# Inverting the recurrent core's triangular blocks by two 64-row quarters of the array instead of one 128-row whole

## What is computed

```
def step(state, inp):
    r_t, w_t, k_t, v_t, kk_t, b_t = inp
    sa = jnp.einsum('bhvk,bhk->bhv', state, -kk_t)
    state = state * w_t[..., None, :] + sa[..., None] * b_t[..., None, :] + v_t[..., None] * k_t[..., None, :]
    return state, jnp.einsum('bhvk,bhk->bhv', state, r_t)
```

## Time and profile before

| | us |
|---|---|
| median of 3 runs (1482.71 to 1483.98) | 1483.03 |
| the profiled execution | 1483.33 |
| its span | 1481.5 |
| recurrent core, chunk 0, first input matmul to right side | 874.02 to 914.14 |
| recurrent core, chunk 1, the same | 926.70 to 966.33 |
| first expert matmul | 1039.83 |
| PE busy in the span | 1421.2 (96%) |

### The profile page before, as it was taken

The page is one execution under the profiler, slowest core; times in us unless marked ns, Lnnn a source line. Parts: engine busy times, 40 slices in busy tenths (PEclk is TensorE's granted clock), DMA queues, the critical chain, the costliest instruction groups (busy, mean ns, idle before and its releaser), DMA issues.

```text
span 1481.5 us, 19431 instructions
## 1 busy us (share of the span) xinstructions
PE 1421.2 (96%) x7478; PEld 1005.4 (68%) x7478; DVE 638.6 (43%) x1060; ACT 543.6 (37%) x814; POOL 446.0 (30%) x302
## 2 busy tenths in 40 slices
PE   8999999999999999999999999998999999999898
PEld 7888888888788888887787679965444344344343
DVE  5664544445664554354158654744222022022021
ACT  6666543445666634334455422212111111111111
POOL 2472544444372544545868220100000000000000
PEclk9999999999999999999999999999999999999999
DMA  7341455454341455456764600128999999999997
GB/s 272 129 164 58 143 206 192 174 202 160 129 164 58 143 193 204 170 191 230 243 226 130 242 0 13 51 114 356 375 430 430 426 428 428 427 428 427 429 424 296
DMA packets 50248, 351.95 MB, mean 238 GB/s; under 512 B 7747, under 2 KB 9679, under 8 KB 25583
## 3 DMA queue, kind: packets, MB, share of 16 engines
q1 hardware_dynamic: 49438, 349.52, 61.0%
q10 hardware_dynamic: 720, 1.20, 0.2%
HBM read 347.78 MB, written 1.07 MB: 235 GB/s over the span
## 4 chain that ended last, share of the span: by engine, by line
PE 74%; DMA 9%; issue 6%; DVE 4%; ACT 3%; POOL 2%; DVEq 1%; SPq 1%; POOLq 0%; ACTq 0%
PE psum L1813 12%; PE psum L1101 10%; PE psum L1103 10%; PE psum L1102 10%; PE psum L1393 8%; DMA ring<-in_w_expert_up 8%; PE psum L1837 5%; PE psum L1395 4%; PE psum L1091 3%; PE psum L1742 2%; PE psum L1752 2%; PE psum L1222 1%; DMA weights_raw<-in_second_w 1%; PE psum L1608 1%; POOL weights_split L913 1%
## 5 line engine op out<-in xcount | busy, mean ns | idle before, releaser
L913 POOL TENSOR_TENSOR weights_split<-weights_raw,weights_split 128x512 fp32r<-128x512 f32 (+2 forms) x253 | 395.7, 1596 | 361.3 <-ACT weights_split L1919 361.2
L1919 ACT ACTIVATE weights_split<-weights_raw 128x2048 fp32r<-128x2048 f32 (+4 forms) x154 | 243.5, 1587 | 254.6 <-PE psum L1103 149.4
L1813 PE MATMUL psum<-ring,arena 128*64 128x512 f32 x960 | 225.0, 594 | 17.6 <-DMA ring<-in_w_expert_up 12.5
L1393 PE MATMUL psum<-h_split,weights_split 128*128 128x512 f32 x512 | 181.2, 398 | 1.4 <-DVE weights_split L913 1.4
L1813 PEld LDWEIGHTS psum<-ring,arena 128*64 128x64 f32 x960 | 72.9, 137 | 145.1 <-issue 141.2
L1101 PE MATMUL psum<-weights_split,h_split 128*128 128x512 f32 (+3 forms) x400 | 152.1, 380 | 6.4 <-POOL weights_split L913 4.9
L1101 PE MATMUL psum<-weights_split,hidden_split 128*128 128x512 f32 (+1 forms) x384 | 151.5, 394 | 0.0
L913 DVE TENSOR_TENSOR weights_split<-weights_raw,weights_split 128x2048 fp32r<-128x2048 f32 (+3 forms) x53 | 119.5, 2259 | 71.2 <-ACT weights_split L1919 69.4
L1103 PE MATMUL psum<-weights_split,h_split 128*128 128x512 f32 (+3 forms) x400 | 149.9, 375 | 0.0
L1102 PE MATMUL psum<-weights_split,h_split 128*128 128x512 f32 (+3 forms) x400 | 149.7, 374 | 0.0
L1103 PE MATMUL psum<-weights_split,hidden_split 128*128 128x512 f32 (+1 forms) x384 | 148.0, 385 | 0.0
(11 more groups left out here) (381 smaller groups left out, 1888.5 us busy)
## 6 DMA issues: line engine op xcount, KB each, us to landing
weights_raw<-in_layer_w SPq DMA_DIRECT2D x94, 1024.0 KB, 4.8
arena<-in_w_expert_down SPq DMA_DIRECT2D x28, 2048.0 KB, 16.5
ring<-in_w_expert_up SPq DMA_DIRECT2D x28, 2048.0 KB, 16.7
ring<-in_w_expert_gate SPq DMA_DIRECT2D x24, 2048.0 KB, 16.3
weights_raw<-in_second_w SPq DMA_DIRECT2D x44, 512.0 KB, 5.1
ring<-in_w_expert_up SPq DMA_DIRECT2D x8, 1024.0 KB, 12.7
arena<-in_w_expert_down SPq DMA_DIRECT2D x16, 512.0 KB, 11.5
arena<-in_w_expert_gate SPq DMA_DIRECT2D x3, 2048.0 KB, 9.2
```

What stands on the lines that cost most here:

```text
L913: ins = eng.tensor_tensor(W.part(j, 1, n)[:, cols], W.raw(j, n)[:, cols], W.part(j, 0, n).bitcast(F32)[:, cols], ALU.subtract)
L1393: pe.matmul(both.rearrange("p (w s) -> p w s", w=2), w[0][:, k, f * P:(f + 1) * P], hTp[:, :, k, :], start=(k == 0), stop=False)
L1813: ins = pe.matmul(bank[half(j), :], xe[h][:, k, half(j)], w[j][:, k, :], start=(k == 0), stop=(k == KD - 1))
L1919: act.activation(W.part(j, 0, w), W.raw(j, w), ACT.Copy).then_inc(W.hi, 1)
```

## The change

The inverse is built for two diagonal blocks of 64 tokens (`HALF`) at once, and the two are joined at the end.

- `T`, `TT` and `X` shrink to 4 heads x 64 columns: rows 0 to 63 hold the upper diagonal block, rows 64 to 127 the lower. Each product over them (`by_blocks`) is eight matmuls of 64 rows by 64 weights columns by 64 columns, alternately on rows and output partitions 0 to 63 and on 64 to 127, into one bank. Each is a quarter of the array; the two lie on its diagonal.
- Turning `T` is now such a matmul with the identity, not a transpose, and is done at every level, the first too.
- `LEVELS` has five entries instead of six. A last step joins the blocks: `XF` (4 matmuls), a last `TT`, and `XT` (4 matmuls); ACT writes the diagonal blocks and DVE the upper right one into `NT`, which then serves L1682 as `TT` served L1642 before.
- Units of the inputs are made for both `par` together, with the matmuls alternating between the two row halves and two banks (`core_inputs`). `N` (`core_diagonals`) makes only the diagonal blocks. `Mak`, `Mrb` and `Mrk` (`LATE_INPUTS`) move behind the `X` and `TT` units of levels 0, 1 and 2, and their masks on DVE likewise.
- POOL's three operations per `par` go; DVE masks `N` and adds the identity itself.

```
-LEVELS = [2 ** i for i in range(1, 7)]
+LEVELS = [2 ** i for i in range(1, 6)]
+HALF = P // 2
+LATE_INPUTS = ("Mak", "Mrb", "Mrk")
...
+                for c in range(PAIRS):
+                    for par in range(2):
+                        r = slice(RW_E * par, RW_E * (par + 1))
+                        ins = pe.matmul(banks[par][:, c * P:(c + 1) * P], left_m[r, c, tok], right_m[r, c, tok], start=True, stop=True)
...
+            def by_blocks(bank, left, right):
+                for c in range(PAIRS):
+                    for rows in blocks:
+                        ins = pe.matmul(bank[rows, at(c)], left(rows, c), right(rows, c), start=True, stop=True)
+                return ins
...
+                def turned_inverse(n, i, m):
+                    bank = units.begin(("TT", 8 * n + i))
+                    units.finish(("TT", 8 * n + i), by_blocks(bank, lambda rows, c: m["T"][rows, c, :], lambda rows, c: ident[rows, rows]))
...
                 for i in range(len(LEVELS)):
                     for par in range(2):
                         n, m = 2 * t + par, core[par]
...
+                        inverse_ready(n, i)
+                        units.wait_emptied(("NT", n))
                         bank = units.begin(("X", 8 * n + i))
...
+                        units.finish(("X", 8 * n + i), by_blocks(bank, lambda rows, c: m["NT"][rows, c, rows], lambda rows, c: m["T"][rows, c, :]))
+                        turned_inverse(n, i, m)
+                    if i < len(LATE_INPUTS):
+                        core_inputs(t, LATE_INPUTS[i])
                     for par in range(2):
                         n, m = 2 * t + par, core[par]
...
+                        units.wait_emptied(("X", 8 * n + i), ("TT", 8 * n + i))
+                        bank = units.begin(("T", 8 * n + i))
+                        units.finish(("T", 8 * n + i), by_blocks(bank, lambda rows, c: m["TT"][rows, c, :], lambda rows, c: m["X"][rows, c, :]))
...
-            eye = ident.unsqueeze(1).to_broadcast([P, PAIRS, P])
-            for n, (t, par) in enumerate(CORE):
-                m = core[par]
-                pool.wait_ge(core_masked, n + 1)
-                pool.tensor_tensor(m["TT"], m["NT"], second("level1T").unsqueeze(1).to_broadcast([P, PAIRS, P]), ALU.mult)
-                pool.tensor_tensor(m["T"], m["T"], eye, ALU.add)
-                pool.drain()
-                pool.tensor_tensor(m["TT"], m["TT"], eye, ALU.add).then_inc(core_start, 1)
...
                 for i in range(len(LEVELS)):
...
+                    level = second("levels")[:, i * HALF:(i + 1) * HALF]
                     for par in range(2):
                         key = ("X", 8 * (2 * t + par) + i)
...
+                        units.emptied_by(key, dve.tensor_tensor(core[par]["X"], bank, every(level), mul), "V")
+                    if i < len(LATE_INPUTS):
+                        masked_inputs(t, LATE_INPUTS[i])
                     for par in range(2):
...
+                        key, a = ("T", 8 * (2 * t + par) + i), core[par]["T"]
+                        units.emptied_by(key, dve.tensor_tensor(a, over_pairs(units.wait_full(key), HALF), a, add), "V")
                     if t == 1:
                         head_norm(0, i)
```

More of the change, by code:

```diff
@@ new lines, in _, with core_diagonals @@
+            blocks = [slice(HALF * b, HALF * (b + 1)) for b in range(2)]
+            at = lambda c: slice(c * HALF, (c + 1) * HALF)
+            def core_diagonals(t):
+                A, B = rwT[0:2]
+                banks = [units.begin(("N", 2 * t + par)) for par in range(2)]
+                for c in range(PAIRS):
+                    for b, rows in enumerate(blocks):
+                        tok = slice(t * P + HALF * b, t * P + HALF * (b + 1))
+                        for par in range(2):
+                            r = slice(RW_E * par, RW_E * (par + 1))
+                            ins = pe.matmul(banks[par][rows, at(c)], A[r, c, tok], B[r, c, tok], start=True, stop=True)
+                            if c == PAIRS - 1 and b == 1:
+                                units.finish(("N", 2 * t + par), ins)
@@ new lines, in _ @@
+                upper, lower = blocks
+                for par in range(2):
+                    n, m = 2 * t + par, core[par]
+                    inverse_ready(n, len(LEVELS))
+                    bank = units.begin(("XF", n))
+                    for c in range(PAIRS):
+                        ins = pe.matmul(bank[lower, at(c)], m["NT"][upper, c, lower], m["T"][upper, c, :], start=True, stop=True)
+                    units.finish(("XF", n), ins)
+                    turned_inverse(n, len(LEVELS), m)
@@ L1611, in value @@
+                for par in range(2):
+                    n, m = 2 * t + par, core[par]
+                    units.wait_emptied(("XF", n), ("TT", 8 * n + len(LEVELS)))
+                    bank = units.begin(("XT", n))
+                    for c in range(PAIRS):
+                        ins = pe.matmul(bank[upper, at(c)], m["X"][lower, c, :], m["NT"][lower, c, lower], start=True, stop=True)
+                    units.finish(("XT", n), ins)
                 def value(c, par):
@@ L2782, in gate_rw, with masked_inputs @@
                 dve.tensor_tensor(a, a, g, add).then_inc(mixed, 1)
-            every = lambda name: second(name).unsqueeze(1).to_broadcast([P, PAIRS, P])
+            every = lambda table: table.unsqueeze(1).to_broadcast([P, PAIRS, table.shape[1]])
+            over_pairs = lambda bank, w: bank[:, 0:PAIRS * w].rearrange("p (c s) -> p c s", c=PAIRS)
+            def masked_inputs(t, name):
+                for par in range(2):
+                    bank = over_pairs(units.wait_full((name, 2 * t + par)), P)
+                    mask = second("minus_strict" if name in ("NT", "Mak") else "incl")
+                    units.emptied_by((name, 2 * t + par), dve.tensor_tensor(core[par][name], bank, every(mask), mul), "V")
@@ L2785, in _ @@
             for t in range(T):
+                if t == 0:
+                    gate_att(0)
                 for par in range(2):
[L2787 to L2799, removed]
+                    bank = over_pairs(units.wait_full(("N", 2 * t + par)), HALF)
+                    units.emptied_by(("N", 2 * t + par), dve.tensor_tensor(core[par]["T"], bank, every(second("minus_level1")[:, 0:HALF]), mul), "V")
@@ L2838, in _ @@
             gate_rw(1)
-            for step in range(3, len(LEVELS)):
+            for step in range(3, len(LEVELS) + 1):
                 head_norm(1, step)
```

126 lines of the change are left out of this document (67 added, 59 removed).

## The result

The changed kernel takes 1470.88 us (median of 4, 1465.70 to 1472.43) against 1482.87 (4, 1481.12 to 1483.98): a ratio of 0.9909, 95% interval 0.9889 to 0.9930. Repeated beside the last experiments it took 1471.25 (6) against 1482.08 (12), 0.9920 (0.9904 to 0.9937). So it is faster by 12 us, inside the range of 1456 to 1474 but outside the forecast's own case of 1457 to 1467, with a little over half of the 21 us that were forecast.

The account below looks back on a forecast made before the run. PE's pace was taken to bound the core. Chunks of 28.4 and 29.1 us, together 57.5 against 79.75, save 22.2 us, less 1.2 for shape changes: 21.0 off 1483.33 gives 1462 us, range 1456 to 1474.

Parts of the forecast that it names:

- the forecast's own case: Whole kernel: the core saving arrives as priced, giving 1457 to 1467 us; chance 0.67.
- The saving moves all that follows: From core to experts: a saving in the core starts the expert loads earlier by the same amount, one for one.
- PE's pace: Products by blocks in the core: two tiles overlap at 28 ns an instruction, so a unit of 16 takes 0.50 us.
- Rival 4: Expert loads: the gain is made and lost because the experts begin earlier but wait for DMA; 1483 us; chance 0.04.
- Rival 1: Products by blocks: no overlap between the quarters, a unit takes 0.90 us, gain 1 us, 1482 us; chance 0.10.
- the quarter at 112 ns: Products by blocks: a quarter matmul goes like L1571, units 1.79 us, stage 136 us, 1540 us; within the 0.05 slower case.
- The levels: Core levels: 4.84 us with a late input, 3.27 without, 4.05 for the last such level in chunk 1.
- the 1.2 set aside for changes of shape: Late units in the core: 12 changes of instruction shape, about 0.1 us each, deduct 1.2 us from the gain.
- what stands ahead of level 0 in chunk 1: Start of chunk 1's core: masks and sums without a projection as cover, 3.43 us in the sum.
- Rival 3: Whole core: PE at half pace, units 0.94 us, stage 88.3 us, 1492 us; chance 0.05.
- rival 2: Behind the joins: the clock falls in part, 1.7 us each, with a level or two slowed by 2.5; 1466 to 1472; chance 0.14.
- the case of 0.45 us a unit: Products by blocks at the lower bound: stage 55.4 us, a gain of 24.4 us, 1459 us.

Follow-up runs that it names:

- tiles in turn: Changed kernel with each product by blocks doing its four upper quarters first, then its four lower ones: 1472.47 us, ratio 0.9931 to the kernel before the change.
- joins filled: Changed kernel with 128x256 matmuls into a bank nobody reads, in the gaps where PE waits in the join: 1464.43 us, ratio 0.9876 to the kernel before the change.
- kernel after: The kernel with the whole change, against the kernel before it: 1470.88 us, ratio 0.9909; repeated, 1471.25 us, ratio 0.9920.

## Why the prediction was right, and where its gain was too high

- *The saving moves all that follows.* Right: the expert load and the first expert matmul came 17.1 us earlier, and the experts took 441.7 us before and 440.9 after. Rival 4 fell.
- *PE's pace.* 0.50 us a unit forecast, 0.47 measured. The two quarters overlap though they write one bank (on different partitions); tiles in turn show 54 to 58 ns within a quarter, as the stream of 64 columns gave. Rival 1 and the quarter at 112 ns fell. The rule of the Trainium skill's "TensorEngine Tiling (Array Packing)", "Gotcha 1: PSUM Pressure", that different row tiles cannot access one bank at the same time, does not agree with this trace: 16 instructions on two row tiles and one bank in 0.47 us. `N` was priced too high: its matmuls alternate over all four quarters, not two, and 32 of them took 869.61 - 868.98 = 0.63 us, 20 ns each, where 28 were forecast.
- *The levels.* 4.84 forecast and 4.88 measured, with the masks before the sum as the last to end. Chunk 0: 28.4 and 28.2. Chunk 1: 29.1 and 29.7. Together 57.5, or 58.7 with the 1.2 set aside for changes of shape, against 57.9. A late unit does take 1.10, where 0.90 and 0.12 were forecast. The agreement of the sums is partly luck: what stands ahead of level 0 in chunk 1 took 3.87 for 3.43 and the joins 3.8 and 4.2 for 3.6 and 3.9, while in chunk 0 the two levels without a late input took 6.15 for 6.54. Rival 3's half pace through the whole core did not come. How much of the cores' 21.8 us each part of the change gives, five levels, quarters or POOL's part, is read from these terms; no run takes one of them out of the changed kernel.
- *The failed step* is the one that priced the clock: "one fall behind each join slows 3.4 us of dense work by half, 1.7 us", with 0.14 of the chance. It had the joins right as a place, and both the chance and the size wrong. The falls are the usual case here, ten of twelve joins and not one in seven, and they last 6.8 and 13.7 us (10.2 for the second when repeated), so that they cost 3.3 and 6.4 us and not 1.7 each. With the joins filled, all of it came back. I had argued from "about 2 us busy in 3.7"; it was 2.61 and 2.15 of 3.40, busier than the stretch of 1.79 that I compared with, and the clock fell all the same. The other stretch of the earlier trace rows, 1.80 busy, had none behind it, as the row behind it shows, so that the busy time of a thin stretch did not tell the two cases apart even then:

```profile
424.30:427.70 3.40, 3.40 (x24) 3.14 (x25) 0.96 (x3) 0.14 (x1) 3.40 (x4) 1.00 0.77 231
```

- *A thin place that it missed.* The prediction priced 3.4 us ahead of level 0 in chunk 1, without cover for DVE's masks, but not the clock there; five of the eleven profiles of the changed kernel and its variants (starred above, at 917 to 924 us) have a fall there, behind 1.3 to 1.9 us busy in 3.40. In the later levels, which it took as safe with "3.9 of 4.8 us busy", no fall of any profile begins.
- *How long the falls last* is open. Behind the joins PE is busy nearly all through the falls, with matmuls of 64 columns (L1670, L1682) and with projections; in the kernel after, the clock came back among the 64-column matmuls of L1682 the first time (905.0) and in a projection (L1094) the second (956.2). No run changed that work.
- *The likeliest time* was therefore 9 us too low: 1462 forecast, 1471 measured, which is rival 2's 1466 to 1472. That total agrees in part by luck: rival 2 made it of 1.7 us a join and of levels slowed by 2.5 each, where 3.3 and 6.4 were measured with no level slowed. The time lies in the stated range because the range took in rival 2.
- *Small slips* of the working, none of which moves the forecast: the case of 0.45 us a unit leaves out the 1.2 us for changes of shape, with which it gives 1460 and not 1459; the terms of a level with a late input add up to 4.83; and the thirteen slices of the earlier trace rows begin at 1000 us, not at 1037, with 356 and 375 GB/s in the first two and 296 in the last.

## What to carry to other kernels

When a chain of small matmuls is cut short, look at what the engine does while it waits for the shorter steps: a gap that was filled by slow work may now let the clock fall, and the dense work behind it pays. In this kernel that was the usual case (ten of twelve joins, 3.4 to 13.7 us at half clock), so price it, look at every place where PE waits, the start of a stage too, and try a few useless matmuls in the gaps. Moving work "into gaps" helps only if each engine that it needs has the gap: here PE had one, and DVE, which had to mask the result before the sum, had not.

## What the runs showed that I had not expected

- PE overlaps tiles across instruction order: with four matmuls of one half in a row and then four of the other it still ran the neighbours in pairs (1.64 us for two units, where 1.8 would be none and 1.10 is all; units of 0.58 instead of 0.9).
- Adding 2.4 us of useless matmuls took 6.4 us off the kernel, and quarters did it about as well as whole ones (1464.9 against 1464.4).
- The clock fell behind waits of PE that were short: none in the joins of the kernel after was over 1.1 us.
- The executions of the kernel after spread by 7 us (1465.7 to 1473.0, ten of them) and those of the one before by 9 (1477.3 to 1486.7), and the profiles differ in where the clock falls; the one profiled execution alone, 1465.7 against 1483.33, would have put the gain at 17.6 instead of 12.
